# Encoder trunk on one core: the short block of keys as one rounded pass over stacked high and low parts

## What is computed

```python
h = rms_norm(x);  p = h @ w_in                     # columns split among the branches
# A: 4 heads, two softmax maps each:  w = softmax(q0 k0) - lam * softmax(q1 k1);  o = w @ v
# B: 4 query heads on 2 key/value heads:  o = softmax(q k) @ v
# C: 4 heads, low-rank queries, keys and values: o = softmax(q k) @ v
# D: pooling mixer (no keys)
y = concat(A, B, C, D) * silu(gates)
x = x + y @ w_out
```

## Time and profile before

| | |
|---|---|
| median of 3 runs | 904.36 us |
| the profiled execution | 904.16 us |
| its span, first to last instruction | 902.4 us |
| PE busy | 895.9 us, 99% |
| DVE busy | 639.7 us, 71% |
| ACT busy | 566.5 us, 63% |
| POOL busy | 0.2 us |
| granted TensorE clock | 1.0 of full speed |

### The profile page before, as it was taken

One profiled execution on the slowest core, in us unless ns is written; L12 is line 12 of the kernel. 1 busy time (PEld: TensorE's weight loads), 2 busy tenths in 40 slices (PEclk: granted clock), 3 DMA queues, 4 the chain that ended last, 5 costly groups with the idle time before them and its releaser, 6 DMA issues.

```text
span 902.4 us, 18072 instructions
## 1 busy us (share of the span) xinstructions
PE 895.9 (99%) x7070; PEld 860.1 (95%) x7070; DVE 639.7 (71%) x1074; ACT 566.5 (63%) x986; POOL 0.2 (0%) x4
## 2 busy tenths in 40 slices
PE   8999999999999999999999999999999999999998
PEld 7999998998999999999999999999999999999998
DVE  7786887678777776766665659877787667766552
ACT  7678756577666667745554588556686666665331
POOL 0000000000000000000000000000000000000000
PEclk9999999999999999999999999999999999999999
DMA  8653343332434343444455543334424344445561
GB/s 339 259 213 140 129 144 125 136 135 104 153 134 149 132 157 119 155 150 186 164 199 187 188 183 145 125 115 182 141 98 183 141 141 162 149 157 187 187 217 64
DMA packets 22996, 143.83 MB, mean 159 GB/s; under 512 B 2560, under 2 KB 4736, under 8 KB 6528
## 3 DMA queue, kind: packets, MB, share of 16 engines
q1 hardware_dynamic: 22768, 142.64, 43.7%
q10 hardware_dynamic: 144, 0.04, 0.0%
HBM read 140.58 MB, written 2.10 MB: 158 GB/s over the span
## 4 chain that ended last, share of the span: by engine, by line
PE 97%; ACT 1%; DMA 1%; SPq 0%; DVE 0%; issue 0%; ACTq 0%; DVEq 0%
PE dense L737 27%; PE dense L739 26%; PE dense L738 26%; PE s_ps L908 4%; PE o_ps L944 4%; PE norm_ps L863 2%; PE t_ps L923 2%; DMA raw<-w_stream_dram 1%; ACT w_hi L1040 1%; PE norm_ps L739 0%; PE swap_ps L739 0%; PE swap_ps L737 0%; PE norm_ps L737 0%; PE norm_ps L738 0%; PE swap_ps L738 0%; PE norm_ps L952 0%
## 5 line engine op out<-in xcount | busy, mean ns | idle before, releaser
L737 PE MATMUL dense<-h_hi,w_hi 128*128 128x272 f32 (+2 forms) x1440 | 426.8, 296 | 1.4 <-DVE h_lo L1329 1.3
L739 PE MATMUL dense<-h_hi,w_lo 128*128 128x272 f32 (+2 forms) x1440 | 412.7, 287 | 0.0
L738 PE MATMUL dense<-h_lo,w_hi 128*128 128x272 f32 (+2 forms) x1440 | 410.9, 285 | 0.0
L1349 DVE TENSOR_TENSOR w_lo<-raw,w_hi 128x1024 fp32r<-128x1024 f32 (+1 forms) x256 | 312.1, 1219 | 85.7 <-ACT w_hi L1040 79.3
L1040 ACT ACTIVATE w_hi<-raw 128x1024 fp32r<-128x1024 f32 (+1 forms) x256 | 270.3, 1056 | 70.0 <-PE dense L739 56.1
L737 PEld LDWEIGHTS dense<-h_hi,w_hi 128*128 128x128 f32 x1440 | 271.3, 188 | 6.8 <-issue 2.8
L738 PEld LDWEIGHTS dense<-h_lo,w_hi 128*128 128x128 f32 x1440 | 271.4, 188 | 1.2
L739 PEld LDWEIGHTS dense<-h_hi,w_lo 128*128 128x128 f32 x1440 | 271.0, 188 | 0.0
L737 PE MATMUL dense<-y_hi,w_hi 128*128 128x272 f32 (+1 forms) x500 | 143.6, 287 | 0.2
L739 PE MATMUL dense<-y_hi,w_lo 128*128 128x272 f32 (+1 forms) x500 | 142.7, 285 | 0.0
L738 PE MATMUL dense<-y_lo,w_hi 128*128 128x272 f32 (+1 forms) x500 | 142.4, 285 | 0.0
(11 more groups left out here) (175 smaller groups left out, 808.9 us busy)
## 6 DMA issues: line engine op xcount, KB each, us to landing
raw<-w_stream_dram SPq DMA_DIRECT2D x128, 1024.0 KB, 4.8
out_dram<-x SPq DMA_DIRECT2D x8, 256.0 KB, 5.3
x<-xt_dram SPq DMA_DIRECT2D x3, 544.0 KB, 9.0
raw<-w_stream_dram SPq DMA_DIRECT2D x3, 512.0 KB, 7.7
con<-consts_dram SPq DMA_DIRECT2D x1, 984.0 KB, 7.4
x<-xt_dram SPq DMA_DIRECT2D x2, 272.0 KB, 4.8
raw<-w_stream_dram SPq DMA_DIRECT2D x2, 256.0 KB, 4.6
d_w<-consts_dram SPq DMA_DIRECT2D x2, 256.0 KB, 5.1
```

The lines of the kernel that those rows point to most:

```text
L737: nc.tensor.matmul(ps, whi, xhi, start=first, stop=False)
L738: nc.tensor.matmul(ps, whi, xlo, start=False, stop=False)
L739: return nc.tensor.matmul(ps, wlo, xhi, start=False, stop=last)
L1349: signal(nc.vector.tensor_tensor(w_lo[:, g % RING, 0:n], raw[:, e % RAW, CHUNK * half:CHUNK * half + n], w_hi[:, g % RING, 0:n].bitcast(F3 ...
```

## The change

The third matmul of each sum is replaced. The tail of the probabilities is copied to `p_tail` in float32; ScalarE writes it rounded into rows 0 to 31 and again into rows 64 to 95 of a new tile `p_parts` (float32r), and VectorE writes the rest, value minus rounded value, into rows 32 to 63. The tail of the values is laid out to match in `v_parts`: GpSimd copies it rounded into rows 0 to 31 and 32 to 63 and writes value minus rounded value into rows 64 to 95. One matmul over these 96 rows then gives high x high + low x high + high x low.

`p_out` is moved from 0.56 to 0.105 in ScalarE's list, and the order in it is: tail, its rounded copy (`p_high`), long blocks (`pt_ready`), second rounded copy (`p_doubled`). `p_low` is new in VectorE's list at 0.48. `pv` waits for `v_parted` instead of `v_ready` or `up_taken`, and ahead of the first short block for `p_doubled` and `p_low_ready`.

```diff
-                 y_split=0.66, xscale=0.283, sub_pre=0.439, x_out=0.55, p_out=0.56, gate=0.65, s_exp=0.579,
+                 y_split=0.66, xscale=0.283, sub_pre=0.439, x_out=0.55, p_out=0.105, gate=0.65, s_exp=0.579,
-AT_VECTOR = dict(sq_sum=0.2, ...
+AT_VECTOR = dict(p_low=0.48, sq_sum=0.2, ...
+AT_POOL = dict(v_out=AT_SCALAR["v_out"], up_out=AT_SCALAR["up_out"])
...
             at(s + 3, ("p_out", l, n))
+            at(s + 3, ("p_low", l, n))
...
-    p_t = sb("p_t", [128, 5, 144])
+    p_t = sb("p_t", [128, 4, 144])
+    p_tail = sb("p_tail", [32, 144])
+    p_parts = sb("p_parts", [96, 144], F32R)
+    v_parts = sb("v_parts", [96, 512], F32R)
...
-                for b in range(3):
-                    mm = nc.tensor.matmul(o_ps[:, c:c + nq], v_st[:, b, v_columns(vh)],
-                                          p_t[:, 4 if b == 2 else 2 * m + b, 0:nq], start=b == 0, stop=b == 2)
+                for b in (0, 1):
+                    nc.tensor.matmul(o_ps[:, c:c + nq], v_st[:, b, v_columns(vh)], p_t[:, 2 * m + b, 0:nq],
+                                     start=b == 0, stop=False)
+                if m == 0:
+                    pe.wait_ge(p_doubled, k + 1)
+                    pe.wait_ge(p_low_ready, k + 1)
+                mm = nc.tensor.matmul(o_ps[:, c:c + nq], v_parts[:, v_columns(vh)], p_parts[:, 0:nq],
+                                      start=False, stop=True)
...
-            link(nc.scalar.activation(p_t[:, 0:n, at_q:at_q + nq],
-                                      t_ps[:, 0:128 * n].rearrange("p (b q) -> p b q", b=n)[:, :, 0:nq], ACT.Copy))
-            signal(nc.scalar.activation(p_t[0:32, 4, at_q:at_q + nq], turned_tails(b, nq), ACT.Copy), pt_ready, k + 1)
+            at = slice(at_q, at_q + nq)
+            link(nc.scalar.activation(p_tail[:, at], turned_tails(b, nq), ACT.Copy))
+            signal(nc.scalar.activation(p_parts[0:32, at], p_tail[:, at], ACT.Copy), p_high, k + 1)
+            signal(nc.scalar.activation(p_t[:, 0:n, at_q:at_q + nq],
+                                        t_ps[:, 0:128 * n].rearrange("p (b q) -> p b q", b=n)[:, :, 0:nq], ACT.Copy),
+                   pt_ready, k + 1)
+            signal(nc.scalar.activation(p_parts[64:96, at], p_tail[:, at], ACT.Copy), p_doubled, k + 1)
...
+        def v_parts_of(c):
+            link(nc.gpsimd.tensor_copy(v_parts[0:32, c], v_st[0:32, 2, c]))
+            link(nc.gpsimd.tensor_copy(v_parts[32:64, c], v_st[0:32, 2, c]))
+            nc.gpsimd.tensor_tensor(v_parts[64:96, c], v_st[0:32, 2, c], v_parts[0:32, c].bitcast(F32),
+                                    ALU.subtract).then_inc(v_parted, 1)
...
+        def p_low(l, n):
+            ...
+            dve.wait_ge(p_high, k + 1)
+            signal(nc.vector.tensor_tensor(p_parts[32:64, at], p_tail[:, at], p_parts[0:32, at].bitcast(F32),
+                                           ALU.subtract), p_low_ready, k + 1)
```

More of the change, by code:

```diff
@@ L129 @@
 AT_SCALAR = dict(rope_fin=-0.166, lat_fin=0.07, mix_out=0.09, lat_pre=0.097, sub_fin=0.1, rope_pre=0.11,
-                 y_split=0.66, xscale=0.283, sub_pre=0.439, x_out=0.55, p_out=0.56, gate=0.65, s_exp=0.579,
+                 y_split=0.66, xscale=0.283, sub_pre=0.439, x_out=0.55, p_out=0.105, gate=0.65, s_exp=0.579,
                  lift=0.6, up_out=0.705, up_next=0.715, split=0.71, x_square=0.72, y_gate=0.73, y_lat=0.74, lam_exp=0.793, v_out=1.297)
-AT_VECTOR = dict(sq_sum=0.2, rope_mid=0.25, rope_turn=0.65, s_max=-0.418, lam_dot=-0.35, sub_fin=-0.345, rope_fin=-0.34, lat_fin=0.055, head_out=0.17,
+AT_VECTOR = dict(p_low=0.48, sq_sum=0.2, rope_mid=0.25, rope_turn=0.65, s_max=-0.418, lam_dot=-0.35, sub_fin=-0.345, rope_fin=-0.34, lat_fin=0.055, head_out=0.17,
                  y_split=0.75, pool=0.266, xscale=0.283, gate=0.7, s_scale=0.491, x_out=0.512, rescale=0.55,
                  x_add=0.614, split=0.71, lam_out=0.82, y_gate=0.76, y_lat=0.72)
+AT_POOL = dict(v_out=AT_SCALAR["v_out"], up_out=AT_SCALAR["up_out"])
 MOVED = {**{("lift", l, 3, 0): -0.55 for l in range(DEPTH)}, **{("split", l, 18): -0.98 for l in range(DEPTH)},
@@ L391, in build @@
     turned_v, v_ready = sem("turned_v"), sem("v_ready")
+    v_parted, p_high, p_low_ready, pool_own = sem("v_parted"), sem("p_high"), sem("p_low_ready"), sem("pool_own")
+    p_doubled = sem("p_doubled")
     gate_exp, gate_done = sem("gate_exp"), sem("gate_done")
@@ L511, in build @@
             mid_no[stg[1:]] = len(mid_no) + 1
+    parted_no, pool_plan = {}, make_plan(AT_POOL)
+    for stg in pool_plan:
+        if stg[0] == "v_out":
+            parted_no[stg[1:]] = len(parted_no) + 1
+        if stg[0] == "up_out" and stg[2:] == (4, 2):
+            parted_no[(stg[1], "c")] = len(parted_no) + 1
     n_scaled = {(l, *PAIRS[p], j): n for (l, p, j), n in scaled_no.items()}
@@ L934, in pv @@
             if branch == "c":
-                pe.wait_ge(up_taken, sum(UP_TILES) * (l + 1))
+                pe.wait_ge(v_parted, parted_no[(l, "c")])
             else:
-                pe.wait_ge(v_ready, v_no[(l, "av", h) if branch == "a" else (l, "bv", 1)])
+                pe.wait_ge(v_parted, parted_no[(l, "av", h) if branch == "a" else (l, "bv", 1)])
             if o_before[k]:
@@ L1231, in _, with link, v_out, up_out @@
         for stage, *what in scalar_plan:
+            if stage in run:
+                run[stage](*what)
+    @block.gpsimd
+    def _(pool):
+        own = [0]
+        def link(ins):
+            own[0] += 1
+            ins.then_inc(pool_own, 1)
+            pool.wait_ge(pool_own, own[0])
+        def v_parts_of(c):
[3 more added lines that the diff above has]
+                                    ALU.subtract).then_inc(v_parted, 1)
+        def v_out(l, kind, i):
+            pool.wait_ge(v_ready, v_no[(l, kind, i)])
+            v_parts_of(v_columns(i))
+        def up_out(l, c, j):
+            if (c, j) == (4, 2):
+                pool.wait_ge(up_taken, sum(UP_TILES) * (l + 1))
+                v_parts_of(slice(0, 512))
+        run = dict(v_out=v_out, up_out=up_out)
+        for stage, *what in pool_plan:
             if stage in run:
@@ L1256, in setup @@
             link(nc.vector.memset(v_st[:, 2, :], 0.0))
-            link(nc.vector.memset(p_t[:, 4, :], 0.0))
             link(nc.vector.memset(odd_only[:, :], 1.0))
@@ L1501, in pool @@
                                                   ALU.mult, ALU.subtract), pooled_ready, n + 1)
+        def p_low(l, n):
+            k = step_no[(l, n)]
+            _, b, h, i = score_steps(l)[n]
+            at = slice(place_in_p_t(l, i), place_in_p_t(l, i) + query_tiles(l)[i][1])
+            dve.wait_ge(p_high, k + 1)
+            signal(nc.vector.tensor_tensor(p_parts[32:64, at], p_tail[:, at], p_parts[0:32, at].bitcast(F32),
+                                           ALU.subtract), p_low_ready, k + 1)
         def s_max(l, n):
@@ L1531, in _ @@
                    lat_fin=lat_fin, sub_fin=sub_fin, head_out=head_out, y_split=y_split, gate=gate, pool=pool,
-                   s_max=s_max, s_scale=s_scale)
+                   p_low=p_low, s_max=s_max, s_scale=s_scale)
         waited = [False]
```

## The result

The changed kernel takes 934.48 us, the median of five runs (930.53 to 934.79), against 904.19 for the kernel before in the same comparison: a ratio of 1.032 (1.031 to 1.033). That is 30 us slower. The direction was forecast, but with 16 us instead of 30, and the stated range ended at 926. The profiled execution has a span of 932.7 us where the kernel before has 902.4. Part of the loss differs between executions of the same kernel: the one of 930.53 us shows a mean granted TensorE clock of 0.994, the one of 931.8 shows 0.993, and the three of 934.5 to 934.8 show 0.991, 0.991 and 0.989. What follows is read from the profiled one, at 934.48 us and 0.991.

What follows compares the result with a forecast made beforehand. TensorE was taken as the bound: 904.16 us, minus 5.7 for shorter passes, plus 21.5 for waits on p_low, plus 0.3 for a late square, gave 920.3 us (16 us slower, 1.8%). The 8-in-10 range was 908 to 926.

Steps and rivals of the forecast that it cites:

- the sum: Whole kernel: 904.16 us less 5.7 for passes, plus 21.5 for p_low waits, plus 0.3 for a late square, gives 920.3.
- TensorE is the bound, and the order of VectorE's list makes it wait: TensorE, busy 895.9 of 902.4 us, would wait for p_low, which stands behind split, pool and rope_mid in VectorE's list.
- The saving of the passes, 5.7 us: At 48 short-block matmuls, one rounded pass of 0.11 us replaces a float32 pair of 0.223 or 0.245; bounds 5.3 to 8.3.
- The sign that was named for it: In the changed profile, 48 short-block matmuls of one record each, with the next record 0.11 us behind.
- The waits, 21.5 us in 16 places: TensorE waits for p_low before the short block in 16 of 32 sums, 0.05 to 3.28 us each, 21.5 in all.
- The wait of 0.44: Sixth of the late sums listed for layer 0: TensorE would wait 0.44 us there for p_low.
- The lag is renewed: Between late sums VectorE waits for TensorE, so its distance returns and the p_low waits add up to 21.5 us.
- the two rivals against it: VectorE's lag is paid once: 901.8 us, chance 0.10; or half of it is renewed: 909.5 us, chance 0.12.
- ScalarE's list is hidden but for 0.3 us: p_out's up to 0.66 us more on ScalarE hides behind its waits for TensorE, except 0.3 us at one place.
- the square that was named: At the fourth sum of layer 1, a square delayed behind p_out holds up the statistics matmul by 0.3 us.
- GpSimd at nothing: GpSimd's three instructions per head's values cost no time: the tightest deadline leaves 8.95 us, 3 us each.
- The port cost of up to 3 us: GpSimd and two-input VectorE instructions lock each other out of a shared SBUF port: at most 3 us more, 923.

Runs made afterwards that it cites:

- second: Changed kernel with the p_low subtraction made by GpSimd, at p_out's place in the list, instead of VectorE, computation complete: 902.05 us, ratio 0.9975.
- third experiment: Changed kernel with p_low at 0.24 instead of 0.48 in VectorE's list, ahead of rope_mid and pool but not of split: 919.45 us, ratio 1.0155.
- seventh: Changed kernel without p_low, plus two more rounded passes of zeros behind each of the 48 short blocks: 911.01 us, ratio 1.0071.
- ninth: Kernel with p_low on GpSimd, with one rope_pre step moved 0.01 ahead so its square stands before p_out again: 900.96 us, ratio 0.9962.
- the idle copies: Kernel with p_low on GpSimd, with idle GpSimd copies put ahead of p_low at 6 sums (944.72 us) or at all 32 (945.15 us).

## Where the prediction was right, and where it failed

The step that failed is the sum. It charged the waits for `p_low` with 21.5 us and let TensorE run at its old pace around them; it had no term for the clock, which came to 7.6 us. The waits themselves were priced 3.4 us too low, and the small waits elsewhere, put at 0.3, were 2.2.

- **TensorE is the bound, and the order of VectorE's list makes it wait.** Right. The first experiment removes `p_low` and with it the loss, and the second keeps the work and moves it off VectorE's list: 902.05 for 934.48 us.
- **The saving of the passes, 5.7 us.** Right: the sums are 5.5 us shorter. The pass takes 0.100 to 0.115 us, against 0.11 taken from the transposes. The sign that was named for it isn't there: the next record follows 0.14 us behind the new matmul (117.40, 117.54), not 0.11, since the matmul itself follows its predecessor sooner.
- **The waits, 21.5 us in 16 places.** Right in kind, but mis-sized. That the brackets hold 21.4 us (in 15 places, the smallest 0.05) is in part luck: the prediction's sum runs from start to start, and so measured the waits cost 24.9. Of the 3.4 us more, 1.5 are the hand-over: 0.05 us were read from ScalarE's copy, and 0.15 are there from the end of VectorE's subtraction to the matmul, at all fifteen waits. Another 1.3 are that TensorE is at the short block sooner: 0.36 to 0.40 us behind the sum's first record, where 0.45 and 0.49 were taken. VectorE itself is where the forecast has it at the first sum: `p_low` ends 2.16 us behind the sum's start in both (117.25 - 115.09, and 116.19 - 114.03 in the forecast). It is 0.9 us later than forecast at the fourth sum (1.75 for 0.85) and 0.4 at the last late one. At the fourth VectorE has no gap between 164.49 and 172.63; which of its instructions put it further back than TensorE I did not separate. The wait of 0.44 didn't occur.
- **The lag is renewed.** Right, and the two rivals against it fall: in the third experiment the five waits behind `split` that come after the removed ones keep their lengths to 0.01 us.
- **ScalarE's list is hidden but for 0.3 us.** Mis-sized: 2.2 us came as small waits elsewhere, of which 0.74 is the square that was named, at 0.3. Squares and `pt_ready` had been looked at, but not the scaled probabilities (`s_scale`, 0.68 and 0.44 at `t_ps`) and a product's output (0.38).
- **GpSimd at nothing.** Right: 26 us of work, never last. The port cost of up to 3 us didn't come: `w_lo` has the same mean, 1219 ns, before and after. Single instructions can pay on either side, as the second experiment shows, but in the changed kernel GpSimd is seldom busy and its work isn't urgent.
- **What was missed altogether: the clock.** No term of the sum and no rival had it, and it is 7.6 us. The view that held it was on the table: the granted clock was 1.0 in a kernel in which TensorE stands for no more than 0.3 us at a time once the opening is over, and the forecast itself introduced seven waits of 1.7 us and more. In that kernel the only stretch at the lower clock after the opening stands where TensorE has stopped for good. That was a reason to give the clock a rival and a wider range.
- **The 14 us between 920.3 and 934.5** are thus 7.6 for the clock, 3.4 for the waits' true cost (24.9 for 21.5), 1.9 for the other waits (2.2 for 0.3), 0.2 for the passes and 1.1 for the opening.

That the lower clock comes from the waits is shown by the runs: it is absent where they are absent (first, second, seventh and ninth experiments, granted clock 1.0) and there with every wait of 3.5 us and more. It isn't seen behind any shorter than 1.69. What decides for waits between there and 2.6 us stays open: of two waits of 2.54 and 2.53 us in the changed kernel the first had it and the second hadn't, one of 1.69 us had it in the third experiment and the same wait of 1.70 hadn't in the changed kernel. It isn't a property of the place alone, since the executions of one kernel differ in it (916.79 us at a clock of 1.000 and 920.58 at 0.996 in the third experiment).

## What to carry to other kernels

When an operand of the bounding engine is moved to another engine, compare the two lists in time at each place, from start to start, and add the hand-over and the loss at the lower clock to each wait: 21 us of idle time cost 33 here. A small instruction for which TensorE waits belongs, in this kernel, on the engine that has nothing long ahead of it and nothing urgent behind it, even if it takes nearly three times as long there (0.80 for 0.28 us). And a small saving is soon used up: a wait cost 2.2 us here on average, with all that came with it (32.5 us for fifteen), so the 5.5 us saved would have carried two of them.

## What the runs showed of the hardware

- TensorE went to the lower of its two clocks with waits as short as 1.7 us, in kernels in which it is busy for 97 to 99% of the time, and stayed there for 3.4 or 6.8 us; each such stretch cost about 1.4 to 3.1 us. Not every wait of 1.7 to 2.6 us did it, all of 3.5 us and more did, and executions of one kernel differ.
- From the end of VectorE's instruction to the start of the matmul that waits for it 0.15 us go by, and the wait costs 0.24 us more than the idle time in front of the record.
- A rounded pass with 96 rows and 128 or 144 columns costs 0.100 us in sequence, a float32 matmul of 128 columns, with its two records, 0.223.
- GpSimd's subtraction of 32 x 128 takes 0.46 us with VectorE idle and up to 1.54 beside VectorE's two-input subtraction, if VectorE isn't the later one to start. Where GpSimd was first, VectorE's subtraction took 1.37 us for 1.23. The mean of all hides that: 1219 ns in both kernels, 1221 with GpSimd's subtraction, 1225 and 1231 with the idle copies before it.
